# First layer of a conditioned decoder: a new order of weight blocks, conditioning and small loads

## What is computed

```python
for l in range(DEPTH):                                   # DEPTH = 2, D = 1024
    sh1, sc1, gt1, sh2, sc2, gt2 = split(silu(c) @ ada_w[l] + ada_b[l], 6)
    h = rmsnorm(x, norm1_g[l]) * (1 + sc1) + sh1         # 256 prompt rows, 64 sample rows
    z = h @ w_in[l]                                      # columns: u 512, v 512, p 512
    u, v = gelu(z[:512]), head_layernorm(gelu(z[512:1024]))
    ya = u * (tril(sgu_w[l]) @ v + sgu_b[l])             # four heads, chunks of 128 (samples: 8)
    d = window_means(p, 2, 4, 8, 16) - p                 # samples start from state_pool[l]
    yb = (d @ pool_w[l]) * pool_scale[l]
    x = x + gt1 * (concat(rmsnorm(ya), rmsnorm(yb)) @ w_out[l])
    h = rmsnorm(x, norm2_g[l]) * (1 + sc2) + sh2
    x = x + gt2 * (dense_swiglu(h) if l == 0 else top2_of_8_swiglu(h))
```

## Time and profile before

| | us |
|---|---|
| median of 3 runs (lowest, highest) | 1563.94 (1563.69, 1564.25) |
| span of the profiled execution | 1561.9 |
| TensorE busy in that span | 1524.3 |
| VectorE, ScalarE, GpSimd busy | 1184.8, 950.2, 88.1 |
| `lo` of one unit, `hi` of one unit | 2.29, 1.90 |
| `lo_pair`; VectorE's copy of one bank of gates | 0.82; 0.69 |
| first product of block (0, 0) starts at | 29.58 |
| last product of the sixth block ends at | 110.1 |

### The profile page before, as it was taken

The page is one execution under the profiler, slowest core; times in us unless marked ns, Lnnn a source line. Parts: engine busy times, 40 slices in busy tenths (PEclk is TensorE's granted clock), DMA queues, the critical chain, the costliest instruction groups (busy, mean ns, idle before and its releaser), DMA issues.

```text
span 1561.9 us, 21723 instructions
## 1 busy us (share of the span) xinstructions
PE 1524.3 (98%) x8071; PEld 1294.5 (83%) x8071; DVE 1184.8 (76%) x960; ACT 950.2 (61%) x730; POOL 88.1 (6%) x131
## 2 busy tenths in 40 slices
PE   6899999999999999999999999999999999999997
PEld 3678899999987788888888888888888888888885
DVE  3466544444466777888888888888888889888997
ACT  3353433333335547677777777777777777777774
POOL 3200000000001012210000000000000000001001
PEclk9899999999999999999999999999999999999999
DMA  9976854444439578999999999999999999999993
GB/s 346 378 301 249 327 197 158 144 152 149 146 112 380 179 243 290 360 383 382 381 378 384 391 363 382 390 372 382 388 374 375 390 374 377 395 368 382 392 386 128
DMA packets 234495, 493.07 MB, mean 316 GB/s; under 512 B 10171, under 2 KB 16187, under 8 KB 229322
## 3 DMA queue, kind: packets, MB, share of 16 engines
q1 hardware_dynamic: 226086, 472.82, 82.3%
q0 software_dynamic: 6064, 19.09, 3.3%
q10 hardware_dynamic: 2308, 0.64, 0.2%
HBM read 482.39 MB, written 10.36 MB: 315 GB/s over the span
## 4 chain that ended last, share of the span: by engine, by line
PE 93%; DVE 3%; DMA 1%; issue 1%; ACT 1%; POOL 1%; SPq 0%; DVEq 0%; ACTq 0%
PE ps L1696 20%; PE ps L1698 20%; PE ps L1697 20%; PE ps L2008 4%; PE ps L2009 4%; PE ps L2010 4%; PE ps L2018 2%; PE ps L2019 2%; PE ps L2020 2%; PE ps L1718 2%; PE ps L2152 2%; PE ps L1965 1%; PE ps L1966 1%; PE ps L1967 1%; PE ps L1735 1%
## 5 line engine op out<-in xcount | busy, mean ns | idle before, releaser
L1085 DVE TENSOR_TENSOR w_lo<-raw,w_hi 128x2048 fp32r<-128x2048 f32 x366 | 835.5, 2292 | 173.1 <-ACT w_hi L734 171.7
L734 ACT ACTIVATE w_hi<-raw 128x2048 fp32r<-128x2048 f32 x366 | 701.8, 1918 | 259.2 <-PE ps L1698 159.4
L1696 PE MATMUL ps<-w_hi,split 128*128 128x512 f32 x1392 | 549.3, 395 | 0.6 <-DVE w_lo L1085 0.6
L1698 PE MATMUL ps<-w_hi,split 128*128 128x512 f32 x1392 | 543.0, 390 | 0.0
L1697 PE MATMUL ps<-w_lo,split 128*128 128x512 f32 x1392 | 542.4, 390 | 0.0
L1696 PEld LDWEIGHTS ps<-w_hi,split 128*128 128x128 f32 x1392 | 261.7, 188 | 57.0 <-DVE w_lo L1085 4.3
L1698 PEld LDWEIGHTS ps<-w_hi,split 128*128 128x128 f32 x1392 | 261.4, 188 | 55.2
L1697 PEld LDWEIGHTS ps<-w_lo,split 128*128 128x128 f32 x1392 | 261.9, 188 | 52.1
L2008 PE MATMUL ps<-split,w_hi 128*128 128x320 f32 x448 | 139.5, 311 | 1.9 <-DVE split L1190 1.9
L2010 PE MATMUL ps<-split,w_lo 128*128 128x320 f32 x448 | 139.2, 311 | 0.0
L2009 PE MATMUL ps<-split,w_hi 128*128 128x320 f32 x448 | 139.1, 311 | 0.0
(11 more groups left out here) (345 smaller groups left out, 1295.8 us busy)
## 6 DMA issues: line engine op xcount, KB each, us to landing
raw<-in_moe_w SPq DMA_DIRECT2D x336, 1024.0 KB, 7.4
raw<-in_ffn_w SPq DMA_DIRECT2D x42, 1024.0 KB, 5.0
raw<-in_ada_w SPq DMA_DIRECT2D x40, 1024.0 KB, 8.6
raw<-in_w_in SPq DMA_DIRECT2D x12, 1024.0 KB, 11.3
raw<-in_ada_w SPq DMA_DIRECT2D x16, 512.0 KB, 10.2
raw<-in_w_out SPq DMA_DIRECT2D x8, 1024.0 KB, 6.7
item_rows<-plain POOLq DMA_DIRECT2D x12, 512.0 KB, 7.8
plain<-in_x_prompt SPq DMA_DIRECT2D x2, 512.0 KB, 4.1
```

The lines of the kernel that those rows point to most:

```text
L734: a.activation(w_hi[:, (s0 + j) % SPL], raw[:, (u0 + j) % RAW], ACT.Copy).then_inc(hi_ready, 1)
L1085: v.tensor_tensor(w_lo[:, (s0 + j) % SPL], raw[:, (u0 + j) % RAW], w_hi[:, (s0 + j) % SPL].bitcast(F32), ALU.subtract).then_inc(lo_ready, 1)
L1696: t_.matmul(out, a_hi, b_hi, start=first_, stop=False)
L1698: return t_.matmul(out, a_lo, b_hi, start=False, stop=last_)
```

## The change

For layer 0 the order of units becomes: FIRST_A, (0, p), (0, v), FIRST_B, (1, p), (1, v), half of SELF_A, (0, u), the other half, (1, u), half of SELF_B, then w_out's blocks with the rest of SELF_B between them. FIRST_B's units 0 and 1 are multiplied inside the first p block, units 2 and 3 behind it, and the turn of FIRST_B inside the first v block.

`weights_tr` is split: `buffer_tr` (pooling state, in bank 7) stands at and in block (1, p); `gates_tr` stands behind `mix_pool(0, 3)`. GpSimd's DMA of the pooling state waits for FIRST_B's last unit, and `load_layer(0)`, the memset of `gs_raw` and the sixteen gate DMAs follow it; the copies of old state and the masks stand behind layer 0's window sums. ScalarE's gate weight DMA stands behind `ada_rows(FIRST_B)`. `gw_raw` and `gs_raw` now share memory with the squares and rows of x, and with uT and v_norm. The functions named `project_in` are split into one for each layer; that of layer 1 is the old one, but for two waits of TensorE (`p_out`, `v_out`) that now stand behind two conditioning units, not ahead of them. `in_products(l, j, w, k)` is the old inner body for row tile k of block j. The diff, cut to its core (removed lines that stand in the functions above are left out):

```diff
+IN_ORDER = [[(0, 0), (0, 1), (1, 0), (1, 1), (0, 2), (1, 2)], [(0, 0), (1, 0), (0, 1), (1, 1), (0, 2), (1, 2)]]
+FIRST_MIXER = [("ada", 4), ("in", 0, 2), ("ada", 4), ("in", 0, 2), ("ada", 4), ("in", 0, 1), ("ada", 4), ("in", 0, 1),
+               ("ada", 4), ("out", 0, 1), ("ada", 2), ("out", 0, 1), ("ada", 2), ("out", 0, 2)]
+NEXT_MIXER = [("in", 1, 1), ("ada", 6), ("in", 1, 1), ("ada", 2), ("ada", 2), ("in", 1, 1), ("ada", 2), ("in", 1, 1),
+              ("ada", 2), ("in", 1, 1), ("ada", 2), ("in", 1, 1), ("out", 1, N_OUT)]
+PARTS = FIRST_MIXER + [("ffn", 0, 2), ("ada", 8), ("ffn", 0, N_FFN - 2)] + NEXT_MIXER
...
+TURN_BANK = [5, 7, 5, 1, 5, 5, 5]
...
+        def load_first_mixer():
+            load_ada(FIRST_A, 0, 4)
+            load_in(0, 0)
+            load_in(0, 1)
+            load_ada(FIRST_B, 0, 4)
+            load_in(0, 2)
+            load_in(0, 3)
+            load_ada(SELF_A[0], 0, 4)
+            load_in(0, 4)
+            load_ada(SELF_A[0], 4, 8)
+            load_in(0, 5)
+            load_ada(SELF_B[0], 0, 4)
+            load_out(0, 0)
+            load_ada(SELF_B[0], 4, 6)
+            load_out(0, 1)
+            load_ada(SELF_B[0], 6, 8)
+            load_out(0, 2)
+            load_out(0, 3)
...
+        gp.wait_ge(plain_used, GROUP_AT[FIRST_B + 1])
+        gp.dma_start(buf_raw[0:NSEQ * BUF], d['state_pool'].rearrange("l b r c -> (b r) l c")).then_inc(buf_in, 16)
+        load_layer(0)
         step(g.memset(gs_raw, 0.0))
...
-        gp.wait_ge(row_out, 1)
-        gp.dma_start(buf_raw[0:NSEQ * BUF], d['state_pool'].rearrange("l b r c -> (b r) l c")).then_inc(aux_in, 16)
-        gp.wait_ge(prep_cp, 6)
-        load_layer(0)
-        for l in range(DEPTH):
-            gp.dma_start(o[3][l, :, 0:BUF - TS, :], d['state_pool'][l, :, TS:BUF, :]).then_inc(stored, 16)
-        step(g.affine_select(out=gw[:], in_=gw[:], compare_op=ALU.is_ge, fill=0.0, base=0,
-                             pattern=[[0, DEPTH * H], [1, P]], channel_multiplier=-1))
-        g.affine_select(out=gs[:], in_=gs[:], compare_op=ALU.is_ge, fill=0.0, base=P - NS_TOK,
-                        pattern=[[0, DEPTH * H], [1, NS_TOK]], channel_multiplier=-1).then_inc(masked, 1)
+        gp.wait_ge(prep_cp, 4)
...
             ins.then_inc(win_s, 1)
+            if l == 0:
+                for j in range(DEPTH):
+                    gp.dma_start(o[3][j, :, 0:BUF - TS, :], d['state_pool'][j, :, TS:BUF, :]).then_inc(stored, 16)
+                gp.wait_ge(prep_cp, 5)
+                step(g.affine_select(out=gw[:], in_=gw[:], compare_op=ALU.is_ge, fill=0.0, base=0,
+                                     pattern=[[0, DEPTH * H], [1, P]], channel_multiplier=-1))
+                g.affine_select(out=gs[:], in_=gs[:], compare_op=ALU.is_ge, fill=0.0, base=P - NS_TOK,
+                                pattern=[[0, DEPTH * H], [1, NS_TOK]], channel_multiplier=-1).then_inc(masked, 1)
...
+            act.wait_ge(split_used, s + 4)
+            a.activation(v_gelu[:], ps[:, 4:4 + NBLK, :], ACT.Gelu_apprx_tanh).then_inc(v_out, 1)
+            for gi in range(3):
+                yb_copy(0, gi)
+            state_copy(0)
+            hi_to(s + 6)
+            ada_rows(SELF_A[0])
+            act.wait_ge(prep_tr, 13)
+            pool_norm(0)
...
         hi_to(S_IN[0] + 1)
+        first_affine(0)
+        hi_to(S_IN[0] + 2)
+        ada_rows(FIRST_B)
         act.dma_start(gw_raw, d['sgu_w'].rearrange("l h t s -> t (l h) s")).then_inc(gw_in, 16)
-        first_affine(0)
-        ada_rows(FIRST_B)
-        hi_to(S_IN[0] + 2)
+        hi_to(S_IN[0] + 3)
         first_affine(2)
-        project_in(0)
+        project_in_first()
         mixer(0)
...
-                    lo_to(S_IN[l] + 1 + half)
+                    lo_to(S_IN[l] + 1 + 2 * half)
                     lo_pair(2 * half)
                     lo_pair(2 * half + 1)
+                    if half == 0:
+                        lo_to(S_IN[l] + 2)
...
+        def project_in_first():
+            s = S_IN[0]
+            buffers_in(0)
+            lo_to(s + 4)
+            buffers_in(1)
+            pooled(0)
+            lo_to(s + 5)
+            v_stats(0)
+            gates_in()
+            lo_to(s + 6)
+            v_normed(0)
+            ada_add(SELF_A[0])
...
+        def buffer_tr(l):
             if l == 0:
-                pe.wait_ge(aux_in, 16 * (2 * NSEQ + 1))
-                pe.wait_ge(gw_in, 16)
+                pe.wait_ge(buf_in, 16)
                 pe.wait_ge(mod_add, FIRST_B + 1)
             else:
...
+        def gates_tr():
+            pe.wait_ge(aux_in, 16 * 2 * NSEQ)
+            pe.wait_ge(gw_in, 16)
+            pe.wait_ge(v_out, 1)
+            for h in range(H):
+                t_.transpose(ps[:, 4, h * P:(h + 1) * P], gw_raw[:, h, :], ident[:])
+            for h in range(DEPTH * H):
+                t_.transpose(ps[:, 6, h * NS_TOK:(h + 1) * NS_TOK], gs_raw[0:NS_TOK, h, :], ident[0:NS_TOK, 0:NS_TOK])
+            for h in range(H):
+                ins = t_.transpose(ps[:, 5, h * P:(h + 1) * P], gw_raw[:, H + h, :], ident[:])
             ins.then_inc(prep_tr, 1)
...
+        def project_in_first():
+            s = S_IN[0]
+            w = unit(s)
+            for k in range(KB):
+                if k >= 2:
+                    ada(FIRST_B, k - 2, k - 1)
+                pe.wait_ge(h_ready, k // 2 + 1)
+                ins = in_products(0, 0, w, k)
+            ins.then_inc(split_used, 1)
+            ada(FIRST_B, 2, 4)
+            w = unit(s + 1)
+            for k in range(KB):
+                if k == 1:
+                    ada_tr(FIRST_B)
+                ins = in_products(0, 1, w, k)
+            ins.then_inc(split_used, 1)
+            w = unit(s + 2)
+            buffer_tr(0)
+            for k in range(KB):
+                if k == 2:
+                    buffer_tr(1)
+                pe.wait_ge(h_ready, 2 + k // 2 + 1)
+                ins = in_products(0, 2, w, k)
+            ins.then_inc(split_used, 1)
+            pe.wait_ge(prep_cp, 4)
+            ada(SELF_A[0], 0, 2)
+            w = unit(s + 3)
+            for k in range(KB):
+                if k == 2:
+                    ada(SELF_A[0], 2, 4)
+                ins = in_products(0, 3, w, k)
+            ins.then_inc(split_used, 1)
+            pe.wait_ge(p_out, 2)
+            pe.wait_ge(d_done, 1)
+            pe.wait_ge(layer_in, 64)
+            for gi in range(3):
+                mix_pool(0, gi)
+            ada(SELF_A[0], 4, 6)
+            pe.wait_ge(yb_done, 1)
+            state_rows(0)
+            pe.wait_ge(yb_done, 2)
+            mix_pool(0, 3)
+            gates_tr()
+            ada(SELF_A[0], 6, 8)
+            w = unit(s + 4)
+            pe.wait_ge(st_cp, 1)
+            pe.wait_ge(yb_done, H)
+            for k in range(KB):
+                ins = in_products(0, 4, w, k)
+            ins.then_inc(split_used, 1)
+            pe.wait_ge(prep_cp, 5)
+            ada_tr(SELF_A[0])
+            ada(SELF_B[0], 0, 4)
+            sum_squares(0, 0, H, 4, uT)
+            w = unit(s + 5)
+            for k in range(KB):
+                ins = in_products(0, 5, w, k)
+            ins.then_inc(split_used, 1)
```

More of the change, by code:

```diff
@@ L487, in _ @@
         sp.dma_start(xtok[0:NS_TOK, 2, :], d['x_sample'].rearrange("b t d -> (b t) d")).then_inc(x_in, 16)
[L488 to L492, removed]
+        load_first_mixer()
         w = (d['ffn_w1'][0], d['ffn_w3'][0], d['ffn_w2'][0])
@@ L819, in yb_copy, with p_copies @@
                          scale=vec[:, l, R_PS + gi:R_PS + gi + 1]).then_inc(yb_done, 1)
[L821 to L828, removed]
+        def p_copies(l, used):
+            act.wait_ge(split_used, used)
             a.activation(pp[:, :, PADP:], ps[:, 0:H, 0:NP_TOK], ACT.Copy).then_inc(p_out, 1)
@@ L834, in project_in, with state_copy @@
             a.activation(sps[:, :, NS_TOK:], ps[:, 0:H, NP_TOK - BUF:NP_TOK], ACT.Copy).then_inc(p_out, 1)
[L835 to L846, removed]
+        def state_copy(l):
             act.wait_ge(st_tr, l + 1)
@@ L1211, in norm, with v_stats @@
             lo_pair(3)
[L1213 to L1225, removed]
+        def v_stats(l):
             ve.wait_ge(v_out, l + 1)
@@ new lines, in in_products @@
+        def in_products(l, j, w, k):
+            (r, c), (wh, wl) = IN_ORDER[l][j], w
+            kk = r * KB + k
+            if c == 1:
+                for b in range(NBLK):
+                    tk = slice(VBLK[b], VBLK[b] + P)
+                    ins = mm3(ps[:, 4 + b, :], h_hi[:, kk, tk], h_lo[:, kk, tk], wh[:, k, :], wl[:, k, :],
+                              kk == 0, kk == KD - 1)
+                return ins
+            for m in range(4):
+                mc = slice(m * P, (m + 1) * P)
+                out = ps[:, m, 0:T]
+                t_.matmul(out, wh[:, k, mc], h_hi[:, kk, 0:T], start=(kk == 0), stop=False)
+                t_.matmul(out, wh[:, k, mc], h_lo[:, kk, 0:T], start=False, stop=False)
```

(35 more changed lines are left out.)

205 lines of the change are left out of this document (66 added, 139 removed).

## The result

| | before | after |
|---|---|---|
| median (lowest to highest), 20 runs each, us | 1563.91 (1560.92 to 1565.51) | 1567.22 (1563.49 to 1570.7) |
| profiled execution: its own time, span | -, 1561.9 | 1570.22, 1568.5 |
| GpSimd's window sums start | 66.32 | 74.88 |
| `mix_pool(0, 0)` starts | 73.17 | 81.41 |
| w_out's first product (end of block (1, 2) + 7.7) | 117.82 | 120.52 |

The ratio is 1.0023, 95% interval 1.0017 to 1.003: the change makes the kernel 3.3 us slower, where 8.0 us faster was forecast. The small loads that moved into GpSimd's queue ahead of its window sums made the sums, and so `mix_pool`, later than before.

What follows compares the result with a forecast made beforehand. TensorE bounds the kernel (93% of the chain), its idle time lying in the first layer. 13.4 us removed - 1.85 - 2.3 - 1.2 = 8.05 us, so 1563.94 becomes 1555.9 us; range 1552.4 to 1561.0.

Steps and rivals of the forecast that it cites:

- Waits removed (FIRST_B): TensorE's waits of 0.72 and 2.10 us before FIRST_B's units 2 and 3 go, part of 8.70 us removed.
- A new idle time: TensorE idles 5.16 us ahead of the first product and the clock falls, costing 2.3 us, bounds 0 and 3.1.
- Rival 1: The clock stays up over the 5.16 us idle time, giving 2.3 us more: 1553.6; chance 0.12.
- Pool state: Its DMA, now behind FIRST_B's last unit, lands late for `buffer_tr(0)`: a wait of 1.2 us, too short to cool.
- GpSimd's queue: Pool state, `load_layer`, memset and gate DMAs precede the sums; one stall is in time, both 2.0 us late; taken as 0.
- rival 3: Sixteen issues and a third long stall hold the sums until F + 33.5; `mix_pool` waits 9.7 us: 1568.7; chance 0.05.
- GpSimd's share of the waits removed: The 5.88 us wait before `mix_pool` goes if GpSimd is in time, with 3.1 us of cold clock behind it.
- Second conditioning half: ScalarE's row copy and VectorE's add, gain, scaling, `lo` and `lo_pair` end in time: cost 0, cover 1.6 us.
- gates: Their 16 transposes (1.6 us) only move behind `mix_pool(3)`, and their DMAs are in before TensorE asks: 0.
- weights: SP's waits are new in order; the tightest, SELF_A's unit 5, has 12 us for a landing: 0.
- layer 1: Its code only puts two conditioning units ahead of a wait that TensorE doesn't show there: 0.

Runs made afterwards that it cites:

- SP's queue: Changed kernel with the sixteen gate DMAs issued from SP's queue behind SELF_A's first half, GpSimd only clearing their buffer: 1558.82 us, ratio 0.9975.
- memset first: Changed kernel with the memset of the gate buffer moved ahead of the pool state's DMA in GpSimd's order: 1569.02 us, ratio 1.0038.
- the sums first, the state early and dummies: Changed kernel, window sums ahead of gate memset and DMAs, pool state's DMA behind second row's output, nine throw-away products before the first product: 1553.83 us.
- the run with the gates early: Changed kernel with the memset and sixteen gate DMAs back at GpSimd's start, into a buffer of their own: 1557.53 us, ratio 0.9959.
- both early: Changed kernel with the pool state's DMA behind the second row's output and gate memset and DMAs at GpSimd's start: 1554.85 us, ratio 0.9945.
- nine dummies: Changed kernel with state and gate DMAs early, plus nine throw-away products in TensorE's idle time ahead of the first product: 1553.39 us, ratio 0.9934.
- the state early: Changed kernel with only the pool state's DMA issued early, behind the second row's output, not behind FIRST_B: 1564.31 us, ratio 1.0001.
- the sums first: Changed kernel with gate memset and DMAs behind the window sums, gates_tr behind block (0, 2): 1558.47 us, ratio 0.9969.

## Why the prediction was wrong, step by step

**Waits removed (FIRST_B):** right. No wait for FIRST_B's units is left.

**A new idle time:** right that the clock falls. Sixteen steps of 0.27 for 0.15 are 2.0 us, against 2.3, and with the idle time filled the clock stays up. Rival 1 fell.

**Pool state:** right that it is waited for, too small in size. It landed after 10.2 us and the wait was 1.8, not 1.2. In the five other kernels that have this wait it was 2.2 to 3.1. The forecast's "too short to cool" held behind 1.79 us, but not always behind more: the clock fell behind 2.32, 2.33 and 2.85 us, and stayed up behind 2.24 and 3.11 (SP's queue, memset first), so the length alone doesn't say. Its removal was worth 2.7 us.

**GpSimd's queue, "I take 0": this step failed.** The prediction let one stall, or two of the sizes seen before, stand ahead of the sums, which then start at F + 25.8 at the latest. There were three, 17.9 us together, and the sums started at F + 31.4. So the 5.88 us in front of `mix_pool`, counted as removed with 3.1 us of cold clock behind it, came back as 6.8 us, with 2.1 us of cold clock (three `mix_pool` in 4.07 us, where they took 2.0 with the sums first, the state early and dummies). That is 8.9 us in the trace; the run with the gates early puts it at 9.7. This is rival 3, which was given a chance of 0.05: its three stalls, and its "decides from a start at about F + 29", came true, with 6.8 us of wait where it said 9.7.

With that alone taken out the time is 1557.5, within 1.6 us of the forecast. In the profiled execution of that run the state's wait was 1.1 us longer than forecast, and the cold stretch behind it, some 1.7 us, wasn't in the forecast at all. These two are more than 1.6 us, so the closeness is in part luck.

The step took the stall for an event with a count and two sizes, both from before, and added them up. The trace of before could have told more:

```profile
55.34 0.54 POOL mix L579
```

```profile
mix<-in_v_norm_b POOLq DMA_DIRECT2D x1, 256.0 KB, 8.3
```

`v_norm_b` went out at 55.34 and took 8.3 us, to 63.6; the stall of 7.59 us ended at 64.00. Read so, a stall ends when a load queued ahead has landed. How long it is depends on how long that takes and on when the next issue is asked for, and it can come once for every batch queued. Nothing then forbids a third, and the "against" of rival 3 (neither row reaches it, even added) has no force.

**GpSimd's share of the waits removed** could also be had without the new order. The old order, with only GpSimd's own steps exchanged, got 6.9 us of the 5.9 + 3.1 that the forecast credited to the change for `mix_pool`.

**Second conditioning half, gates, weights, layer 1 at 0:** no wait of these shows in the list of the kernel after. Once the queue is cured, a wait for conditioning weights shows in front of w_out (1.0 us with both early, 1.4 with nine dummies), so the 0 for the weights holds only while something else is late. For layer 1 one thing stays open: the clock fell near 540 us in the profiled executions of after and of the memset-first kernel (granted 0.75 and 0.83 from 540 to 560 us), and not in that of before. It falls a little later in some others (0.83 from 560 to 580 us with both early, 0.69 with SP's queue). How much of the 3.3 us that is in the median wasn't measured; the first layer's 2.7 us are most of it.

**Open** is also what fills GpSimd's queue, and which landing frees it. The pieces fit better than the number of DMAs, by one run.

## What to carry to other kernels

Before moving loads to a queue whose engine also computes, ask what lands when: add to each issue in the trace its time to landing, and see whether idle time among the issues ends at a landing. If so, treat each batch of loads as a wait for the batch ahead of it, not as a fixed price per issue. Put what the critical path needs from that engine ahead of loads that nobody needs yet; here that one exchange got 6.9 us in the old kernel, and what the new block order added to it lies within the intervals.

## What the runs showed of the hardware

- GpSimd stops among its DMA issues, for 4 to 10 us in most cases and for 0.55 us where it asked late, and goes on 0.3 to 0.5 us behind the landing of a DMA issued earlier. It isn't always the same one. In the memset-first run the first stall ended at 53.53, right behind the state (53.2), the oldest, while `pool_w` and `sgu_b`, at 11.5 and 12.3 us to landing, were still out. With the state early the stall ended behind `v_norm_b`, the last of four, 6.5 us after the oldest had landed; and behind the gate DMAs it ends at the landing of the last one issued.
- Sixteen of the same DMAs from SP's queue went out without a gap, at 0.61 us each; on GpSimd's queue each took 0.54, stalls apart.
- Taking one stall away (8.17 us) moved the next up and made it longer (5.60 to 10.15 us). A stall's length in one trace is not the price of the work ahead of it.
- An idle time of 5.15 us ahead of the first product goes with a granted clock of 0.83 from 20 to 40 us in all eight traces that have it. Products that feed nobody hold the clock up (1.00 in the three traces with them), but fourteen of them, five more than fitted, cost what they bring. Between 2.2 and 3.1 us of idle the clock fell in three of five traces, and the longest of the five wasn't among the three.
- GpSimd's mask of 128x1024 took 3.08 us in the kernel after, where VectorE ran a `lo` from 92.15 to 94.43 us beside its start at 92.31. It took 1.10 us with the sums first, where no `lo` ran beside it.
